# Order of the first levels' steps on ScalarE and VectorE during the dv products, in a transformer layer on one core

## Chip, cores and metric

The kernel runs on one core of one Trainium2 chip. The metric is the device time of one execution in microseconds; lower is better. The time before is the median of three runs.

## The reference, cut to what matters

The reference is two transformer blocks on 512 tokens of width 1024. The first has a projection `project(modulate(x, ...), w_in)` of the tokens and of 256 context tokens, cut into queries, keys and values of a gated linear attention (GLA, four heads) and of a differential attention (four heads; dq, dk, dv). The change lies in the GLA part, at the time that the kernel makes dv:

```python
def gla_chunk_scan(q, k, v, g, s0):
    ...
        qc, kc, vc, gc = inp
        cum = jnp.cumsum(gc, axis=2)
        o_inter = jnp.einsum('bhcd,bhde->bhce', qc * jnp.exp(cum), state)
        rel = cum[:, :, :, None, :] - cum[:, :, None, :, :]
        decay = jnp.exp(jnp.where(mask[:, :, None], rel, -jnp.inf))
        attn = jnp.einsum('bhid,bhjd,bhijd->bhij', qc, kc, decay)
        o = o_inter + jnp.einsum('bhij,bhje->bhie', attn, vc)
        last = cum[:, :, -1:, :]
        state = jnp.exp(last[:, :, 0, :, None]) * state + jnp.einsum('bhcd,bhce->bhde', kc * jnp.exp(last - cum), vc)
    ...
```

Both directions of the scan are computed. A score needs a decay that depends on the query and on the key. The kernel works in windows of 128 tokens and halves them in seven levels: at each level the decay from a key to a query in the other half goes through the border of the halves, and is a product of one factor for the key and one for the query, so that the scores of the level are an ordinary matrix product.

## The kernel before, in words

**Products.** TensorE (PE) runs nearly all the time on products of float32 values that are each split in a high and a low part (three matmuls for one). Weights come in units of up to 128x1024 values. SyncE's queue loads a unit into one of four buffers `raw` (line 537) once VectorE has done with the unit four before. ScalarE (ACT) makes the high part (`hi`, line 590), VectorE (DVE) the low part (`lo`, line 1350), two units ahead of PE. These calls stand between the other steps of each engine's program, whose order is written out by hand; each engine works strictly through its own list, and semaphores tie the lists together.

**The dv stage.** `tokens("dv", 2n, ...)` for n = 0 to 3 is one turn each: 36 matmuls of 128x512 (lines 2367 to 2369), two groups of 18. Between them PE has small work for the GLA part, and all of it goes through the PSUM banks 6 and 7, so that each small step waits until the one before has been read out of these two banks:

- after 12 matmuls of turns 1, 2 and 3: `item(j)`, the scores of a level. `item(0)` holds the undecayed scores of the window (line 2564) and the two lowest levels (line 2578); `item(1)` and `item(2)` (line 2564) are the next levels. An item waits for its level keys (semaphore `lmul`) and for banks 6 and 7.
- after 24 matmuls: `turn_keys(n)`, five transposes of decayed keys (line 2527). It waits for the readers of the item's scores.
- after 36 matmuls of turns 1 to 3: `state(n-1)`, twenty products of keys and values (line 2542). It waits for ACT's copies of the turned keys.

**What reads the banks.** The scores of `item(0)` are copied by ACT into the array `AT` (`first_scores`, line 744, two copies). Those of the later items are written over a part of `AT` by DVE under a mask (`item_scores`, line 1585, two predicated copies). The turned keys are copied by ACT (`turned_keys`, lines 737 and 738). The state is read by DVE (`state`, lines 1553 and 1559, five steps).

**What makes a level.** DVE takes four differences of running sums (`level_gaps`, lines 1509 to 1512, tile `Db`), ACT takes an exponential of them (`decays`, line 708), and DVE multiplies by queries and keys (`level_keys`, lines 1570 and 1573, tile `QKl`). Beside it, keys for the state are decayed (`key_decay` on ACT, line 702; `keys_decayed` on DVE, lines 1518 and 1519). `GAPS_AT[n]` is level n + 2, so the differences and the exponential of level n + 2 stand in turn n.

**The order before**, in turns 1 to 3:

- ACT, turn 1: `hi`, `decays(3)`, `first_scores(0)`, `turned_keys(1)`, `key_decay(3)`. Turns 2 and 3: `hi`, `decays(n + 2)`, `turned_keys(n)`.
- DVE, turn 1: `level_gaps(3)`, `lo`, `state(0)`, `keys_decayed(2)`, `level_keys(2)`. Turn 2: `level_gaps(4)`, `lo`, `level_keys(3)`, `item_scores(1)`, `state(1)`, `keys_decayed(3)`. Turn 3: `level_gaps(5)`, `lo`, `level_keys(4)`, `item_scores(2)`, `state(2)`.

After turn 3 ACT copies dv's six banks to `Vd` (line 762), and the dk products follow (lines 2333 to 2335).

Of the kernel before, what the change touches and what calls it, by code (L numbers as in the profile page):

```python
# [194 lines left out]
def build(nc, ap, out):  # L195
# [6 lines left out]
    with ctx:  # L202
# [55 lines left out]
        def bank(b, n=512, c=0):  # L258
            return pall[:, 512 * b + c:512 * b + c + n]
# [8 lines left out]
        def win(a):  # L268
            return a.rearrange("p (w t) -> p w t", t=128)
# [128 lines left out]
        for (_, _, _, cn, _, nk, _) in plan:  # L398
            offs.append(offs[-1] + 128 * cn * nk)
# [81 lines left out]
        ITEM_AT = {1: 0, 2: 1, 3: 2, 4: 3, 5: 4, 6: 5, 8: 6, 9: 7, 10: 8, 11: 9, 12: 10, 13: 11}  # L481
# [5 lines left out]
        def level_at(i):  # L487
            hp, lev = i // 7, i % 7 + 1
            return hp, lev, i % 2 if i < 6 else 2 + i % 2, NI * hp + max(lev - MG, 0)
# [85 lines left out]
        def _(e):  # L575
# [10 lines left out]
            def hi(upto):  # L586
                for j in range(made[0], min(upto + 1, NU)):
                    w.wait_ge(s_raw[j % 4], 16 * (j // 4 + 1))
                    w.wait_ge(s.used, j - 2)
                    e.activation(whi[j % 3][:, 0:cols(j)], raw[j % 4][:, 0:cols(j)], ACT.Copy).then_inc(s.hi, 1)  # L590
                    made[0] = j + 1
# [103 lines left out]
            def key_decay(i):  # L695
                z, hp = i // 2, i % 2
                if z == 0:
                    w.wait_ge(s.kds, hp + 1)
                    e.activation(ktd[:, hp, :], ktd[:, hp, :], ACT.Exp, scale=GN).then_inc(s.kde, 1)
                else:  # L700
                    w.wait_ge(s.kt, hp + 1)
                    e.activation(ktd[:, hp, :], Fc[:, 1, hp, :], ACT.Exp, scale=GN).then_inc(s.kde, 1)

            def decays(i):
                t = level_at(i)[2]
                w.wait_ge(s.lsub, i + 1)
                use_exp()
                e.activation(Db[t][:, :, :], Db[t][:, :, :], ACT.Exp, scale=GN).then_inc(s.lexp, 1)
# [25 lines left out]
            def turned_keys(i):  # L734
                z, hp = i // 2, i % 2
                w.wait_ge(s.kt, i + 1)
                e.activation(ktok[z][:, 0:4, hp, :], win(bank(6)), ACT.Copy).then_inc(s.ktk, 1)
                e.activation(ktok[z][:, 4, hp, :], bank(7, 128), ACT.Copy).then_inc(s.ktk, 1)

            def first_scores(hp):  # L740

                for sub in range(2):
                    w.wait_ge(s.lp, 2 * NI * hp + sub + 1)
                    e.activation(AT[hp][:, sub, :], bank(6 + sub), ACT.Copy, scale=2.0).then_inc(s.lat, 1)
# [3 lines left out]
            for n in range(4):  # L748
                hi(J[("dv", 2 * n)] + 2)
                if n == 0:  # L750
                    turned_keys(0)
                for i in GAPS_AT[n]:
                    decays(i)
                if n == 1:
                    first_scores(0)
                if n:
                    turned_keys(n)
                if n < 2:
                    key_decay(2 + n)
# [29 lines left out]
            for i in range(4):  # L789
                n = 4 + i  # L790
# [42 lines left out]
            for i in range(4):  # L833
                n = 8 + i
# [506 lines left out]
        def _(e):  # L1341
# [4 lines left out]
            def lo(upto):  # L1346
                for j in range(made[0], min(upto + 1, NU)):
                    w.wait_ge(s.hi, j + 1)
                    n = cols(j)
                    e.tensor_tensor(wlo[j % 3][:, 0:n], raw[j % 4][:, 0:n], f(whi[j % 3][:, 0:n]),  # L1350
                                    ALU.subtract).then_inc(s.lo_v, 1)
                    made[0] = j + 1
# [140 lines left out]
            def level_gaps(i):  # L1493
                hp, lev, t, _ = level_at(i)
                D_ = Db[t]
                b = 64 >> (lev - 1)

                def pr(x):
                    return x.rearrange("p (n t b) -> p n t b", t=2, b=b)

                F_, E_ = pr(Fc[:, 0, hp, 0:512]), pr(Fc[:, 1, hp, 0:512])
                rf = F_[:, :, 0, b - 1:b].to_broadcast([128, 256 // b, b])
                rb = E_[:, :, 1, 0:1].to_broadcast([128, 256 // b, b])
                Dq, Dk = pr(D_[:, 0, :]), pr(D_[:, 1, :])
                w.wait_ge(s.tot, 2 + 2 * hp)
                if i >= 6:
                    w.wait_ge(s.up, 4)
                w.wait_ge(s.lmul, i - 1)
                e.tensor_tensor(Dq[:, :, 1, :], F_[:, :, 1, :], rf, ALU.subtract)
                e.tensor_tensor(Dq[:, :, 0, :], rb, E_[:, :, 0, :], ALU.subtract)  # L1510
                e.tensor_tensor(Dk[:, :, 0, :], rf, F_[:, :, 0, :], ALU.subtract)
                e.tensor_tensor(Dk[:, :, 1, :], E_[:, :, 1, :], rb, ALU.subtract).then_inc(s.lsub, 1)

            def keys_decayed(i):
                hp = i % 2
                w.wait_ge(s.kde, i + 1)
                w.wait_ge(s.dn, 4)
                e.tensor_tensor(ktd[:, hp, 0:512], ktd[:, hp, 0:512], qk[:, hp, 1, :], ALU.mult)
                e.tensor_tensor(ktd[:, hp, 512:768], ktd[:, hp, 512:768], kc[:, hp, :], ALU.mult).then_inc(s.kdm, 1)
# [27 lines left out]
            def state(i):  # L1547
                z, hp = i // 2, i % 2
                order = windows[z]
                w.wait_ge(s.up, i + 1)  # L1550
                w.wait_ge(s.dec, 1)
                own = S_[:, z, hp, order[2], :]
                e.tensor_copy(own, bank(6, 128)).then_inc(s.stv, 1)
                for k in range(1, 5):
                    to = own if k == 1 else S_[:, z, hp, order[k + 1], :]
                    frm = own if k <= 2 else S_[:, z, hp, order[k], :]
                    add = bank(6, 128, 128 * k) if k < 4 else bank(7, 128)
                    w.wait_ge(s.stv, 5 * i + k)
                    e.scalar_tensor_tensor(to, frm, dect[:, z, hp, order[k]:order[k] + 1], add, ALU.mult,
                                           ALU.add).then_inc(s.stv, 1)  # L1560

            def level_keys(i):
                hp, lev, t, _ = level_at(i)
                w.wait_ge(s.lexp, i + 1)
                if i >= 2:
                    w.wait_ge(s.lp, 2 * level_at(i - 2)[3] + 2)
                w.wait_ge(s.gq, 2)
                if lev <= MG:

                    e.scalar_tensor_tensor(QKl[t][:, :, :], Db[t][:, :, :], math.sqrt(0.5), qk[:, hp, :, :], ALU.mult,  # L1570
                                           ALU.mult).then_inc(s.lmul, 1)
                else:
                    e.tensor_tensor(QKl[t][:, :, :], Db[t][:, :, :], qk[:, hp, :, :], ALU.mult).then_inc(s.lmul, 1)

            def item_scores(j):
                hp, k = j // NI, j % NI
                if k == 0:
                    return
                for sub in range(2):
                    src, dst = win(bank(6 + sub)), win(AT[hp][:, sub, :])  # L1580
                    w.wait_ge(s.lp, 2 * j + sub + 1)
                    w.wait_ge(s.g_const, 3)
                    w.wait_ge(s.lat, 2 * (j - 1) + sub + 1)
                    m = lmask[:, MG + k - 1, :].unsqueeze(1).to_broadcast([128, 4, 128])
                    e.copy_predicated(dst, m, src).then_inc(s.lat, 1)

            keys_decayed(1)
            for n in range(4):
                if n:
                    for i in GAPS_AT[n]:  # L1590
                        level_gaps(i)
                lo(J[("dv", 2 * n)] + 2)
                if n == 0:
                    level_keys(0)
                    level_keys(1)
                    level_gaps(2)
                if n >= 2:
                    level_keys(n + 1)
                    item_scores(ITEM_AT[n])
                if n:  # L1600
                    state(n - 1)
                if 1 <= n < 3:
                    keys_decayed(n + 1)
                if n == 1:
                    level_keys(2)


            def query_gap(hp):
# [23 lines left out]
            for i in range(4):  # L1632
                n = 4 + i
# [44 lines left out]
            for i in range(4):  # L1678
                n = 8 + i
# [24 lines left out]
            for i in range(4):  # L1704
                n = 12 + i
# [191 lines left out]
            for i in range(4):  # L1897
                lo(J[("zu", i, 0)] + 2)
                w.wait_ge(s.vf, 4 + i + 1)
                cur, n = u[:, i, :], 0  # L1900
# [8 lines left out]
                n = 2 << i  # L1909
# [1442 lines left out]
```

## Time and profile before

| what | us |
|---|---|
| median of three runs (1601.65 to 1602.03) | 1601.9 |
| the profiled execution | 1601.25 |
| span of the profiled execution | 1599.4 |
| PE busy in the span | 1548.7 |
| VectorE busy | 930.6 |
| ScalarE busy | 733.1 |
| GpSimd busy | 120.9 |

The span is the time between the first and the last instruction of the profiled execution; 1.85 us lie around it. The table shows which engine is nearly full. A busy time says nothing about one stage, though: what a step costs is seen in the timeline, where each row is one instruction or some equal ones in a row, and where brackets tell how long the engine stood idle ahead of it and what released it. The rows of the last section are of that kind. The dv stage with the change lies between 118 and 159 us.

### The profile page before, as it was taken

The page shows a single profiled execution, that of the slowest core. Times are in us where ns is not written, and L with a number is a line of the kernel's source. Part 1 is how long each engine was busy: PE and PEld are TensorE (multiplying, and loading weights), DVE is VectorE, ACT ScalarE, POOL GpSimd, SP SyncE. Part 2 cuts the span into 40 slices and gives each one's busy share as a digit, 9 for nine tenths or more (in the row PEclk, how much of TensorE's full clock was granted, in tenths as well). Part 3 has the DMA queues.
Part 4 walks back from the last instruction along what each step waited for, and adds up shares of the span by engine and source line. Part 5 has one row for each costly group of instructions (what it writes and reads, how often), then busy time and mean ns, then how long its engine had stood idle before and what let it go on. Part 6 is the DMA issues. An engine that isn't in the chain of part 4 may idle for free.

```text
span 1599.4 us, 19834 instructions
## 1 busy us (share of the span) xinstructions
PE 1548.7 (97%) x7939; PEld 1250.4 (78%) x7939; DVE 930.6 (58%) x1405; ACT 733.1 (46%) x1158; POOL 120.9 (8%) x89
## 2 busy tenths in 40 slices
PE   8998998989999999999999899999989999999998
PEld 5676876778788888888778677788779888888887
DVE  4765878876644433334646555365757785267745
ACT  5463546774432222323443667455556553244432
POOL 0000214630000000000100111130010000000000
PEclk9999999899999999999999999999999999999999
DMA  9721112105333232223232222143313232333221
GB/s 380 273 93 54 53 54 61 46 4 194 119 132 119 82 121 100 92 68 104 90 109 63 67 73 69 40 145 93 92 44 102 68 118 74 111 106 103 79 86 63
DMA packets 49840, 157.70 MB, mean 99 GB/s; under 512 B 5682, under 2 KB 12466, under 8 KB 49492
## 3 DMA queue, kind: packets, MB, share of 16 engines
q1 hardware_dynamic: 48352, 151.80, 28.9%
q10 hardware_dynamic: 1396, 4.63, 0.8%
q8 instruction: 63, 1.03, 0.3%
q14 instruction: 29, 0.24, 0.0%
HBM read 154.31 MB, written 2.10 MB: 98 GB/s over the span
## 4 chain that ended last, share of the span: by engine, by line
PE 78%; DVE 12%; ACT 8%; issue 2%; POOL 0%; DMA 0%; DVEq 0%; SPq 0%; ACTq 0%
PE pall L2333 18%; PE pall L2334 17%; PE pall L2335 17%; PE pall L2893 2%; PE pall L2894 2%; PE pall L2895 2%; PE pall L2367 1%; PE pall L2368 1%; PE pall L2369 1%; DVE wlo L1350 1%; ACT whi L590 1%; ACT e L908 1%; DVE R L1363 1%; DVE statd L1727 1%; DVE W L1361 1%
## 5 line engine op out<-in xcount | busy, mean ns | idle before, releaser
L1350 DVE TENSOR_TENSOR wlo<-raw,whi 128x1024 fp32r<-128x1024 f32 (+2 forms) x263 | 294.2, 1119 | 291.2 <-ACT whi L590 291.1
L590 ACT ACTIVATE whi<-raw 128x1024 fp32r<-128x1024 f32 (+2 forms) x263 | 247.0, 941 | 179.6 <-PE pall L2335 164.6
L2333 PE MATMUL pall<-h5h,whi 128*128 128x512 f32 x320 | 124.9, 390 | 1.0 <-DVE wlo L1350 1.0
L2335 PE MATMUL pall<-h5h,wlo 128*128 128x512 f32 x320 | 124.5, 389 | 0.0
L2334 PE MATMUL pall<-h5l,whi 128*128 128x512 f32 x320 | 124.5, 389 | 0.0
L2333 PE MATMUL pall<-h2h,whi 128*128 128x512 f32 x320 | 124.5, 389 | 0.0
L2334 PE MATMUL pall<-h2l,whi 128*128 128x512 f32 x320 | 124.5, 389 | 0.0
L2335 PE MATMUL pall<-h2h,wlo 128*128 128x512 f32 x320 | 124.5, 389 | 0.0
L2333 PEld LDWEIGHTS pall<-h5h,whi 128*128 128x128 f32 x320 | 60.1, 188 | 14.1 <-DVE wlo L1350 1.4
L2334 PEld LDWEIGHTS pall<-h2l,whi 128*128 128x128 f32 x320 | 60.1, 188 | 12.6
L2335 PEld LDWEIGHTS pall<-h5h,wlo 128*128 128x128 f32 x320 | 60.1, 188 | 12.5
L2333 PEld LDWEIGHTS pall<-h2h,whi 128*128 128x128 f32 x320 | 60.1, 188 | 12.5
L2335 PEld LDWEIGHTS pall<-h2h,wlo 128*128 128x128 f32 x320 | 60.1, 188 | 12.4
L2334 PEld LDWEIGHTS pall<-h5l,whi 128*128 128x128 f32 x320 | 60.1, 188 | 12.3
L2333 PE MATMUL pall<-fh,whi 128*128 128x512 f32 x176 | 68.5, 389 | 0.0
L2334 PE MATMUL pall<-fl,whi 128*128 128x512 f32 x176 | 68.5, 389 | 0.0
L2335 PE MATMUL pall<-fh,wlo 128*128 128x512 f32 x176 | 68.5, 389 | 0.0
L2333 PE MATMUL pall<-ch,whi 128*128 128x512 f32 x154 | 59.9, 389 | 0.0
L2334 PE MATMUL pall<-cl,whi 128*128 128x512 f32 x154 | 59.9, 389 | 0.0
L2335 PE MATMUL pall<-ch,wlo 128*128 128x512 f32 x154 | 59.9, 389 | 0.0
L996 ACT ACTIVATE fh<-tmp 128x512 fp32r<-128x512 f32 x22 | 13.9, 632 | 95.1 <-DVE tmp L1833 95.1
L2893 PE MATMUL pall<-h3h,whi 128*128 128x512 f32 x120 | 49.6, 414 | 0.3 <-ACT tmp L1071 0.3
(519 smaller groups left out, 3677.6 us busy)
## 6 DMA issues: line engine op xcount, KB each, us to landing
raw<-in_weights SPq DMA_DIRECT2D x204, 512.0 KB, 3.5
mraw<-in_wmod SPq DMA_DIRECT2D x32, 512.0 KB, 4.9
mod<-in_weights SPq DMA_DIRECT2D x16, 512.0 KB, 14.7
raw<-in_weights SPq DMA_DIRECT2D x25, 256.0 KB, 2.6
raw<-in_weights SPq DMA_DIRECT2D x32, 192.0 KB, 2.3
xT<-in_x SPq DMA_DIRECT2D x4, 512.0 KB, 5.4
xT<-in_x ACTq DMA_DIRECT2D x1, 2048.0 KB, 7.6
out_y<-xT SPq DMA_DIRECT2D x5, 256.0 KB, 2.2
```

What stands on the lines that cost most here:

```text
L590: e.activation(whi[j % 3][:, 0:cols(j)], raw[j % 4][:, 0:cols(j)], ACT.Copy).then_inc(s.hi, 1)
L908: e.activation(EB[n % 3][c][:, :], bank(b, 768), ACT.Exp, bias=sd[:, col + 1:col + 2], accum_out=sd[:, col + 2:col + 3]).then_inc(s.ex, 1)
L1350: e.tensor_tensor(wlo[j % 3][:, 0:n], raw[j % 4][:, 0:n], f(whi[j % 3][:, 0:n]), ALU.subtract).then_inc(s.lo_v, 1)
L1361: e.scalar_tensor_tensor(W[:, 0:n], m, EPS * dim, W[:, 0:n], ALU.add, ALU.mult).then_inc(s.rsum, 1)
L1363: e.scalar_tensor_tensor(r, W[:, 0:n], 1.5, r, ALU.subtract, ALU.mult, reverse0=True).then_inc(s.rstd, 1)
L1727: e.reduce_max(sd[:, col + 1:col + 2], bank(2 * dpair[c, n], 768), AX.X, negate=True).then_inc(s.mx, 1)
L2333: e.matmul(o_, a[:, kk, :], xh(k), start=(k == 0), stop=False)
L2334: e.matmul(o_, a[:, kk, :], xl(k), start=False, stop=False)
L2335: mm = e.matmul(o_, b[:, kk, :], xh(k), start=False, stop=(k == nk - 1))
L2893: e.matmul(bank(b), a[:, k, :], xh[:, k, :], start=(k == 0), stop=False)
L2894: e.matmul(bank(b), a[:, k, :], xl[:, k, :], start=False, stop=False)
L2895: mm = e.matmul(bank(b), c[:, k, :], xh[:, k, :], start=False, stop=(k == nk - 1))
```

## The change

It changes no instruction, only the order of some within ACT's and DVE's lists. On ACT, `first_scores(0)` goes ahead of `decays(3)` in turn 1. On DVE, `item_scores(n - 1)` of turns 2 and 3 goes from behind `level_keys` to the head of the turn, ahead of `level_gaps` and `lo`; and `level_keys(2)` of turn 1 goes ahead of `state(0)`. (`ITEM_AT` gives item 1 for turn 2 and item 2 for turn 3.)

```diff
@@ ScalarE
                 if n == 0:
                     turned_keys(0)
+                if n == 1:
+                    first_scores(0)
                 for i in GAPS_AT[n]:
                     decays(i)
-                if n == 1:
-                    first_scores(0)
                 if n:
                     turned_keys(n)
                 if n < 2:
@@ VectorE
             keys_decayed(1)
             for n in range(4):
+                if n >= 2:
+                    item_scores(ITEM_AT[n])
                 if n:
                     for i in GAPS_AT[n]:
                         level_gaps(i)
@@
                     level_keys(0)
                     level_keys(1)
                     level_gaps(2)
-                if n >= 2:
+                else:
                     level_keys(n + 1)
-                    item_scores(ITEM_AT[n])
-                if n:
                     state(n - 1)
                 if 1 <= n < 3:
                     keys_decayed(n + 1)
-                if n == 1:
-                    level_keys(2)
```

## Rows read from the trace of the kernel before

**Rows 1.** The page: PE's, VectorE's and ScalarE's busy time, instructions; weight loads to landing.

```profile
PE 1548.7 (97%) x7939; PEld 1250.4 (78%) x7939; DVE 930.6 (58%) x1405; ACT 733.1 (46%) x1158; POOL 120.9 (8%) x89
...
raw<-in_weights SPq DMA_DIRECT2D x204, 512.0 KB, 3.5
```

**Rows 2.** Stretches: busy us of PE, PEld, DVE, ACT, POOL; granted clock; DMA share, GB/s.

```profile
118.00:159.00 41.00, 36.51 (x330) 28.57 (x328) 23.94 (x45) 14.17 (x23) 0.00 (x0) 1.00 0.16 53
276.00:292.00 16.00, 13.95 (x50) 10.01 (x50) 13.44 (x18) 8.47 (x17) 9.08 (x7) 0.68 0.36 131
```

**Rows 3.** Timeline of PE, dv turns 0 and 1: start us, length, instruction, idle before.

```profile
114.78 0.39 PE L2369 MATMUL pall<-whi,hxl 128*128 128x512 f32 x1
115.01 0.71 PE L2527 MATMUL pall<-ident,ktd 128*128 128x128 f32 x5
115.47 0.47 PE L2367 MATMUL pall<-whi,hxh 128*128 128x512 f32 x1
...
126.16 0.39 PE L2369 MATMUL pall<-whi,hxl 128*128 128x512 f32 x1
128.28 0.74 PE L2527 MATMUL pall<-ident,ktd 128*128 128x128 f32 x5 [1.74 <-ACT AT L744]
128.78 0.48 PE L2367 MATMUL pall<-whi,hxh 128*128 128x512 f32 x1
```

**Rows 4.** Timeline of PE, dv turn 2.

```profile
135.55 0.39 PE L2369 MATMUL pall<-whi,hxl 128*128 128x512 f32 x1
137.09 1.16 PE L2564 MATMUL pall<-QKl 64*128 64x128 f32 x16 [1.15 <-DVE QKl L1573]
...
140.81 0.39 PE L2369 MATMUL pall<-whi,hxl 128*128 128x512 f32 x1
142.02 0.74 PE L2527 MATMUL pall<-ident,ktd 128*128 128x128 f32 x5 [0.83 <-DVE AT L1585]
142.52 0.48 PE L2367 MATMUL pall<-whi,hxh 128*128 128x512 f32 x1
...
145.43 1.31 PE L2542 MATMUL pall<-Vg,ktok 128*64 128x128 f32 x20
```

**Rows 5.** Timeline of PE, dv turn 3.

```profile
149.29 0.39 PE L2369 MATMUL pall<-whi,hxl 128*128 128x512 f32 x1
149.61 1.16 PE L2564 MATMUL pall<-QKl 64*128 64x128 f32 x16
...
153.33 0.39 PE L2369 MATMUL pall<-whi,hxl 128*128 128x512 f32 x1
154.51 0.73 PE L2527 MATMUL pall<-ident,ktd 128*128 128x128 f32 x5 [0.79 <-DVE AT L1585]
155.00 0.47 PE L2367 MATMUL pall<-whi,hxh 128*128 128x512 f32 x1
```

**Rows 6.** Timeline of ScalarE, dv turn 1.

```profile
126.18 1.04 ACT L708 ACTIVATE Db<-Db 128x1024 f32<-128x1024 f32 x1
127.12 1.06 ACT L744 ACTIVATE AT<-pall 128x512 f32<-128x512 f32 x2
129.06 0.60 ACT L737 ACTIVATE ktok<-pall 128x512 f32<-128x512 f32 x1 [0.88 <-PE pall L2527]
```

**Rows 7.** Timeline of VectorE, end of dv turn 1 and turn 2.

```profile
133.05 0.29 DVE L1553 COPY S_<-pall 128x128 f32<-128x128 f32 x1 [5.51 <-PE pall L2542]
133.37 1.50 DVE L1559 SCALAR_TENSOR_TENSOR S_<-S_,tots,pall 128x128 f32<-128x128 f32 x4
...
135.72 1.22 DVE L1573 TENSOR_TENSOR QKl<-Db,qk 128x1024 f32<-128x1024 f32 x1
136.98 0.42 DVE L1509 TENSOR_TENSOR Db<-Fc 128x256 f32<-128x256 f32 x1
...
138.32 1.22 DVE L1350 TENSOR_TENSOR wlo<-raw,whi 128x1024 fp32r<-128x1024 f32 x1
...
140.59 1.33 DVE L1585 COPY_PREDICATED AT<-lmask,pall 128x512 f32<-128x512 uint8 x2
```

## The prediction

> **What bounds the kernel.** I read the page first: PE is busy 97% of the span, the next engine 58% [rows 1]. So a change that touches only ScalarE's and VectorE's order can pay only where PE stands still for them. The second view is the busy time by stretch: in the dv stage, 118 to 159 us, PE works 36.5 of 41 us, at the full granted clock, with DMA 16% busy [rows 2]. Some 4.5 us of standing still are there to be had. The third view is PE's timeline of that stage. It shows four waits of size, at three kinds of work that all go through the banks 6 and 7 [rows 3 to 5]. The fourth and fifth are the timelines of ScalarE and VectorE at the same moments, which show what each releaser was doing before it released [rows 6, 7].
>
> **What a wait costs.** Without a wait the transposes start 0.23 us behind the last matmul, and the next matmul starts 0.46 us behind them (114.78, 115.01, 115.47) [rows 3]. An item starts 0.32 us behind its matmul (149.29, 149.61) [rows 5]. Against this:
>
> - transposes, turn 1: the next matmul at 128.78, and 126.16 + 0.23 + 0.46 = 126.85 without a wait: 1.93 us [rows 3];
> - item 1, turn 2: 137.09 against 135.55 + 0.32 = 135.87: 1.22 us [rows 4];
> - transposes, turn 2: 142.52 against 140.81 + 0.69 = 141.50: 1.02 us [rows 4];
> - transposes, turn 3: 155.00 against 153.33 + 0.69 = 154.02: 0.98 us [rows 5].
>
> In all 5.15 us; the change aims at each of the four.
>
> **Part 1, the first copies ahead of the exponential (ScalarE).** Before, ScalarE starts the exponential of level 3 at 126.18 and the two copies at 127.12. They end at 128.18, and PE's transposes start 0.10 later [rows 3, 6]. The scores are ready long before: the item ran ahead of the 12 matmuls that end the group at 126.16. With the copies first they take the slot from 126.18, end at 127.24, and the transposes start at 127.34 in place of 128.28. Gain 0.94 us; 0.99 of the wait stays, because ScalarE is not free before 126.18. The exponential now ends at about 128.2. Behind it are the copies of the turned keys, which wait for the transposes anyway (127.34 + 0.74 = 128.08), so they start at about 128.15 against 129.06 [rows 3, 6] and keep the gain. Cost on the path: nothing, covered by the transposes; were they done sooner, it would be the exponential's 1.04 at most. The moved exponential feeds level 3's keys, which are wanted ten microseconds later.
>
> **Part 2, level 2's keys ahead of the state (VectorE).** VectorE stands idle 5.51 us ahead of the state at 133.05 [rows 7]. The keys need 1.22 us, and their exponential stands in turn 0, so they fit into the idle time whole and cost nothing. Item 1 on PE, which waited for these keys (they end at 136.94), is then held only by the state's steps, which read the banks: they end at 133.37 + 1.50 = 134.87 before [rows 7], 133.93 after part 1. Item 1 comes at 135.87 - 0.94 = 134.93, 1.0 us behind that, so its whole wait of 1.22 goes. Shift so far 2.16 us.
>
> **Part 3, the masked selections at the head (VectorE).** In turn 2 the selection of item 1 stood behind level 3's differences, the low part of a weight unit and the level's keys, and ended at 140.59 + 1.33 = 141.92, 0.1 ahead of the transposes [rows 4, 7]. Now it waits at the head for item 1: 134.93 + 1.16 = 136.09, plus 0.06 for the signal, and ends at about 137.5. The 12 matmuls end their group so that the transposes can start at 140.81 - 2.16 + 0.23 = 138.88: no wait, with 1.4 us to spare. Gain 1.02, shift 3.18. In turn 3 the same: item 2 at 149.61 - 3.18 = 146.43, selection over by 149.0, transposes at 150.38. Gain 0.98, shift 4.16 us.
>
> **What queues behind the new wait.** The selection is now a wait at the head of the list, and the differences of level 4, a weight unit's low part, and level 3's keys stand behind it. They start at 137.4 instead of 136.98 [rows 7]. The four differences end at 137.4 + 1.43 = 138.8, the exponential (1.06) at 139.9, and ScalarE's copies of the turned keys (0.85, start of the first to end of the second, the second not shown: bounds 0.60 and 1.20, for one or two copies of the length shown [rows 6]) at 140.5 to 141.1. PE wants them for the state at 145.43 - 3.18 = 142.25 [rows 4]. At least 1.1 us remain. Level 3's keys end at about 141.1 and are wanted at 146.4. The low part ends near 140 in place of 139.54, for the first dk unit. PE wanted that at about 159.2 (155.00, plus the 2.91 from transposes to state in turn 2, plus the state's 1.31 [rows 4, 5]), and will at about 155. SyncE's next load waits for that low part and starts 0.4 us later; a load lands 3.5 us after its issue [rows 1], four units ahead of PE. No moved step issues a DMA, and GpSimd has no work in the stage [rows 2].
>
> **Sum.** 0.94 + 1.22 + 1.02 + 0.98 = 4.16 us off the profiled execution's 1601.25, which gives 1597.1. The median of the runs stands 0.65 higher, and I take the gain from it: 1601.9 - 4.2 = 1597.7. At the end of the stage every engine has moved by the same 4.2 us: ScalarE's copies to `Vd`, the last state and the dk products all wait for PE's last dv matmul. So the later stages should keep the shift.
>
> **A clock that could take it or double it.** Between 276 and 292 us the granted clock averages 0.68 [rows 2]. Between the levels 1.0 and 0.5 that is 16 x 0.32 / 0.5 = 10.2 us at the lower one, 1.2 GHz, and PE had stood still several times just before. PE-bound work there loses up to half of it, 5.1 us. The Trainium skill ("TensorE: Matmul & The Clock Gate", "What's actually happening") says that the gate judges PE's activity by its own running time and does not restart with the kernel. By that rule a stage reached 4.2 us sooner could meet the gate otherwise, and the sum could be anything from -9.3 to +0.9. Against a large effect stands that the three runs agree within 0.38 us, so the stretch seems to cost the same each time; I leave the sum at -4.2.
>
> **Rivals.**
>
> 1. *The new head of the turn makes the exponential and the state late.* For it: three steps now hang on PE's item. Against it: 1.1 us of room even at the slow bound. If that room is overrun in both turns so that the 2.0 us of part 3 are given back, 2.16 remain: 1599.7. Chance 0.09.
> 2. *The change does not do what it says, or the gain is absorbed.* A wait put down to the selection could have had a second cause as late, or a later stage with a fixed date could wait longer. The only thing with dates of its own is DMA, at 16% here [rows 2]. Time 1601.9. Chance 0.05.
> 3. *The clock, on the other side.* The stretch at the lower level, now met 4.2 us sooner, grows, or another of PE's waiting stages falls into one. One more stretch of 10.2 us costs 5.1: 1601.9 - 4.2 + 5.1 = 1602.8, slower than before. It decides from 8.3 us more at the lower level on. Two such stretches would give 1607.9. Chance 0.03 for one, 0.02 for two.
> 4. *The clock, in favour.* The stretch does not occur: 1597.7 - 5.1 = 1592.6. Chance 0.03.
>
> **How the numbers follow.** The forecast has 0.78; its own range is 1596.7 (all 5.15 us gone) to 1598.7 (a quarter of the gain lost in signals and pitches). About 0.2%, or 3.2 us, is what a measurement of this kernel can tell from no change. Faster by more than that: forecast and rival 4, 0.81. Within: rivals 1, 2 and the single stretch of 3, 0.17. Slower: 0.02. The range reaches down from 1596.7 by a quarter of the clock's 5.1, to 1595.4, and up to rival 1 with 0.4 for the spread of runs, 1600.1; outside are rivals 2 to 4, some 0.13.
>
> **What would show it.** In the changed profile: transposes of turn 1 still wait, for about 0.8 us, for the copies (line 744), now ahead of the exponential (line 708). Item 1 and the transposes of turns 2 and 3 show no wait. VectorE stands idle at the head of turns 2 and 3, released by line 2564, some 1.2 us. The first dk matmul comes at about 155.1 in place of 159.2. The granted clock between 272 and 288 looks as before between 276 and 292. The prediction is wrong if PE waits ahead of the states (line 2542), if the first dk matmul comes later than 156, or if it comes at 155 and the end does not follow.

## The result, and the profile after

The changed kernel takes 1597.32 us in the median of 8 runs (1595.63 to 1597.57); the kernel before, run beside it, 1601.96 (8 runs, 1601.65 to 1602.74). The ratio is 0.9969, with a 95% interval of 0.9960 to 0.9977: faster by about 0.3%, or 4.6 us, and beyond the 0.2% that the prediction named as the limit. In microseconds the interval reaches from 3.7 to 6.4. The profiled execution took 1597.36 us, with a span of 1595.5 against 1599.4.

The page of the changed kernel, the line that answers to the first of [rows 1]:

```profile
PE 1549.6 (97%) x7939; PEld 1251.3 (78%) x7939; DVE 930.7 (58%) x1405; ACT 732.9 (46%) x1158; POOL 120.5 (8%) x89
```

Its busy time by stretch, the line that answers to the first of [rows 2] (busy us of PE, PEld, DVE, ACT, POOL, then granted clock, DMA share, GB/s):

```profile
118.00:159.00 41.00, 40.21 (x363) 32.09 (x363) 26.37 (x51) 17.42 (x28) 0.00 (x0) 1.00 0.17 53
```

No engine does more or less work over the span, and the granted clock of the stage is 1.00 in both kernels, so the gain there is not one of the clock. In the same 41 us PE is now busy for 40.21 us with 363 matmuls, where it was busy for 36.51 with 330. (The dv products end sooner now, so some of the 363 are dk products.) What is left of its standing still is one wait. PE's timeline, against [rows 3 to 5]:

```profile
115.68 0.71 PE L2525 MATMUL pall<-ident,ktd 128*128 128x128 f32 x5
...
126.83 0.39 PE L2367 MATMUL pall<-whi,hxl 128*128 128x512 f32 x1
128.01 0.74 PE L2525 MATMUL pall<-ident,ktd 128*128 128x128 f32 x5 [0.79 <-ACT AT L744]
...
135.28 0.39 PE L2367 MATMUL pall<-whi,hxl 128*128 128x512 f32 x1
135.59 1.16 PE L2562 MATMUL pall<-QKl 64*128 64x128 f32 x16
...
139.32 0.39 PE L2367 MATMUL pall<-whi,hxl 128*128 128x512 f32 x1
139.55 0.71 PE L2525 MATMUL pall<-ident,ktd 128*128 128x128 f32 x5
...
142.94 1.31 PE L2540 MATMUL pall<-Vg,ktok 128*64 128x128 f32 x20
...
150.86 0.39 PE L2367 MATMUL pall<-whi,hxl 128*128 128x512 f32 x1
151.09 0.71 PE L2525 MATMUL pall<-ident,ktd 128*128 128x128 f32 x5
...
155.78 0.47 PE L2331 MATMUL pall<-hxh,whi 128*128 128x512 f32 x1
```

and the first dk matmul of the kernel before:

```profile
159.21 0.47 PE L2333 MATMUL pall<-hxh,whi 128*128 128x512 f32 x1
```

PE's lines have moved up by two (2527 is now 2525). This execution comes to the stage 0.67 us later than the one of before (115.68 against 115.01), so times are to be compared from there. Item 1 stands 0.31 behind its matmul, the transposes of turns 2 and 3 0.23 behind theirs: no waits. Only the transposes of turn 1 still wait for `first_scores`. From turn 0's transposes to the first dk matmul it was 159.21 - 115.01 = 44.20 us before and is 155.78 - 115.68 = 40.10 now: 4.10 us, where the prediction had 4.16. I call this length the **stage** in what follows; it is how the experiments are compared, since what lies outside it varies by more: over the ten profiles of this document, PE comes to the stage after 114.4 to 116.0 us, and what follows the stage takes between 1439.4 and 1445.6 us. For this pair the span's 3.9 us are 4.10 less in the stage, 0.67 more ahead of it and about 0.5 less behind it.

ScalarE's timeline of the changed kernel, turn 1 and turn 2, against [rows 6]:

```profile
126.85 1.06 ACT L744 ACTIVATE AT<-pall 128x512 f32<-128x512 f32 x2
127.80 1.06 ACT L708 ACTIVATE Db<-Db 128x1024 f32<-128x1024 f32 x1
128.78 0.60 ACT L737 ACTIVATE ktok<-pall 128x512 f32<-128x512 f32 x1
...
139.48 1.06 ACT L708 ACTIVATE Db<-Db 128x1024 f32<-128x1024 f32 x1 [6.85 <-DVE Db L1512]
140.45 0.58 ACT L737 ACTIVATE ktok<-pall 128x512 f32<-128x512 f32 x1
140.93 0.27 ACT L738 ACTIVATE ktok<-pall 128x128 f32<-128x128 f32 x1
```

VectorE's, end of turn 1 and turn 2, against [rows 7]:

```profile
128.12 1.22 DVE L1573 TENSOR_TENSOR QKl<-Db,qk 128x1024 f32<-128x1024 f32 x1
132.77 0.29 DVE L1553 COPY S_<-pall 128x128 f32<-128x128 f32 x1 [3.43 <-PE pall L2540]
...
136.79 1.36 DVE L1585 COPY_PREDICATED AT<-lmask,pall 128x512 f32<-128x512 uint8 x2 [1.26 <-PE pall L2562]
138.03 0.41 DVE L1509 TENSOR_TENSOR Db<-Fc 128x256 f32<-128x256 f32 x1
```

Level 2's keys now sit in VectorE's idle time ahead of the state, and VectorE now stands idle for 1.26 us at the head of the turn, released by PE's item, which costs nothing. ScalarE's copies of the turned keys are over at 141.20, and PE's state begins at 142.94: 1.7 us of room for the chain behind the new wait.

### The profile page after: what moved, and what is told of

It is laid out like the page before. It is cut to its first block, busy times and chain, and to the rows that moved or that the text cites. A ratio compares the mean times of both kernels' runs of the same rounds, so it can differ in the third digit from the quotient of the medians.

```text
span 1595.5 us, 19834 instructions
## 1 busy us (share of the span) xinstructions
PE 1549.6 (97%) x7939; PEld 1251.3 (78%) x7939; DVE 930.7 (58%) x1405; ACT 732.9 (46%) x1158; POOL 120.5 (8%) x89
## 4 chain that ended last, share of the span: by engine, by line
PE 78%; DVE 11%; ACT 8%; issue 2%; POOL 0%; DMA 0%; DVEq 0%; SPq 0%; ACTq 0%
PE pall L2331 18%; PE pall L2333 18%; PE pall L2332 18%; PE pall L2891 2%; PE pall L2365 2%; PE pall L2367 2%; PE pall L2366 2%; PE pall L2893 2%; PE pall L2892 2%; DVE wlo L1350 1%; ACT whi L590 1%; ACT e L908 1%; DVE statd L1725 1%; DVE W L1361 1%; DVE R L1363 1%
```

## The experiments

Eight kernels, the first four on one chip, the other four together on one chip again. On the first chip the runs scattered more (the kernel before: 1600.71 to 1604.26 in 35 runs) than single parts of 1 to 2 us are worth, so the verdict on a part is read from its profile, and the runs stand beside it.

**Part 1 alone.**

```diff
 # the kernel before, ScalarE, turn 1
                 if n == 0:
                     turned_keys(0)
+                if n == 1:
+                    first_scores(0)
                 for i in GAPS_AT[n]:
                     decays(i)
-                if n == 1:
-                    first_scores(0)
```

> Only part 1: the two first copies ahead of the exponential on ScalarE, VectorE's order as before. My account: the transposes of turn 1 come 0.94 us sooner and every later wait stays as it was (1.22 at item 1, 1.02 and 0.98 at the transposes of turns 2 and 3), so PE's first dk matmul comes 0.94 sooner: -0.9 us in the trace and in the runs. Rival (the waits hand over to each other): item 1 still waits for level 2's keys, whose date hangs on something that did not move, and the shift at the dk products is 0.

PE's waits in the stage, 118 to 160 us (who waited, for whom, us in total, how often, the longest):

```profile
PE pall L2527 <- DVE AT L1585: 1.6, 2, 0.8
PE pall L2564 <- DVE QKl L1573: 1.1, 1, 1.1
PE pall L2527 <- ACT AT L744: 0.8, 1, 0.8
```

One wait has shrunk from 1.74 to 0.8, the three others stand as they were. The stage takes 159.26 - 115.99 = 43.27 us: 0.93 off, as expected, and nothing is handed on. The runs (1600.29 against 1601.54, ratio 0.9996, 0.9986 to 1.0005) cannot tell this from no change. The profiled execution itself took 1606.73 us, and what it lost, it lost behind the stage; see the last section.

**Part 2 alone.**

```diff
 # the kernel before, VectorE, turns 1 to 3
+                if n == 1:
+                    level_keys(2)
                 if n:
                     state(n - 1)
                 if 1 <= n < 3:
                     keys_decayed(n + 1)
-                if n == 1:
-                    level_keys(2)
```

> Only part 2: level 2's keys ahead of the state, selection behind level_keys as before, ScalarE as before. My account: item 1 loses its wait of 1.22 us, the transposes of turns 2 and 3 keep theirs (about 1.0 each): -1.2 us. Rival (hand over): the transposes of turn 2 wait 1.2 us longer, since the selection is held by work of VectorE with a fixed date: 0.

The same view:

```profile
PE pall L2527 <- ACT AT L744: 1.7, 1, 1.7
PE pall L2527 <- DVE AT L1585: 1.6, 2, 0.8
```

Item 1's wait is gone, the others are untouched. Stage 157.97 - 115.00 = 42.97: 1.23 off. Runs 1599.85 against 1601.54, ratio 0.9993 (0.9984 to 1.0001): in line with 1.2 us, but not shown by them.

**Part 3 alone.**

```diff
 # the kernel before, VectorE
             for n in range(4):
+                if n >= 2:
+                    item_scores(ITEM_AT[n])
                 if n:
                     for i in GAPS_AT[n]:
                         level_gaps(i)
...
                 if n >= 2:
                     level_keys(n + 1)
-                    item_scores(ITEM_AT[n])
```

> Only part 3: the selections at the head of turns 2 and 3, ScalarE and level 2's keys as before. My account: item 1 waits 1.2 us as before, the transposes of turns 2 and 3 no longer wait: -2.0 us. Rival (the new head of the turn makes the exponential late): PE waits ahead of the states (line 2542) of turns 2 and 3 and the gain is under 1 us, or a loss.

The same view (this file has one line more, so PE's lines are one further down):

```profile
PE pall L2528 <- ACT AT L744: 1.7, 1, 1.7
PE pall L2565 <- DVE QKl L1573: 1.1, 1, 1.1
```

The two waits for the selection are gone, and PE does not wait ahead of a state. Stage 157.24 - 114.94 = 42.30: 1.90 off, 0.1 less than expected. The tenth is spread over both turns (0.96 and 0.94 for 1.02 and 0.98). Runs 1599.65 against 1601.54, ratio 0.9991 (0.9982 to 1.0001).

**Parts 1 and 2.** The edits of the first two experiments together.

> Parts 1 and 2 without the selections at the head. My account: the parts add, 0.94 + 1.22 = 2.16 us off, with waits of about 1.0 us left at the transposes of turns 2 and 3. Rival: they overlap, and one of the two is worth less than 0.5 beside the other.

The same view:

```profile
PE pall L2527 <- DVE AT L1585: 1.6, 2, 0.8
PE pall L2527 <- ACT AT L744: 0.8, 1, 0.8
```

Stage 157.31 - 115.29 = 42.02: 2.18 off. The parts add: 0.93 + 1.23 = 2.16, and with part 3's 1.90 they give 4.06, against 4.10 for all together. The runs (1600.98, ratio 0.9995, 0.9986 to 1.0003) lie higher than the stage says. They reach from 1598.31 to 1603.95 and don't decide anything; that the clock, below, is behind this is not shown.

**The room behind the new wait, two doses.** Products that nobody reads lengthen the chain behind the selection in turns 2 and 3.

```diff
 # the changed kernel, level_gaps (VectorE); the smaller dose has tmp[2:]
                 w.wait_ge(s.lmul, i - 1)
+                for t_ in (tmp[0:] if i in (4, 5) else ()):
+                    e.tensor_tensor(t_[:, :], qk[:, 0, 0, :], qk[:, 0, 1, :], ALU.mult)
                 e.tensor_tensor(Dq[:, :, 1, :], F_[:, :, 1, :], rf, ALU.subtract)
```

> The changed kernel with two more VectorE products of 128x512 (into tmp[2] and tmp[3], which nothing reads) behind the selection and ahead of the differences of levels 4 and 5: the chain selection, differences, exponential, copies of the turned keys is made 1.2 us longer in each of turns 2 and 3. In the changed kernel the copies ended at 141.20 and PE's state began at 142.94, so about 1.6 us of room. My account: hidden, the first dk matmul at the same place as with the change (4.1 us ahead of before, counted from turn 0), no wait ahead of line 2540's counterpart. Rival (the wait at the head of the turn has used the room up): PE waits ahead of the states, 1.2 us per turn, 2.4 in all.

> As before, but four such products per turn, 2.4 us. My account: the room of 1.6 is overrun by 0.8 us in each of the two turns, PE waits ahead of the states of turns 2 and 3 for ScalarE's copies, and the gain of 4.1 at the dk products falls to about 2.5. Rival (the chain is not what ends the state's wait; something else holds it or nothing does): the gain stays 4.1.

PE's waits with the smaller dose:

```profile
PE pall L2527 <- ACT AT L744: 0.8, 1, 0.8
```

and with the larger:

```profile
PE pall L2542 <- ACT ktok L738: 1.5, 2, 0.7
PE pall L2527 <- ACT AT L744: 0.8, 1, 0.8
```

In the profile the two added products take 1.2 us of VectorE's time and the four 2.4. The smaller dose is hidden whole: stage 154.79 - 114.69 = 40.10, the changed kernel's to the hundredth. With the larger, a new wait stands ahead of each of the two states, for ScalarE's copies of the turned keys, as rival 1 described it. The stage is 156.13 - 114.42 = 41.71, so 1.61 of the gain is lost, 0.8 per turn; the gain is 2.49, expected about 2.5. Rival 1 is thus a real mechanism: by these figures it bites once the chain grows by more than some 1.6 us (2.4 less the 0.8 lost), and the change leaves that room. Each dose was run once, with 1597.01 us for the smaller and 1600.37 for the larger: 3.4 us apart where the stages differ by 1.6, so a single run does not measure the dose.

**The copies moved further up.**

```diff
 # the changed kernel, ScalarE
             for n in range(4):
+                if n == 1:
+                    first_scores(0)
                 hi(J[("dv", 2 * n)] + 2)
                 if n == 0:
                     turned_keys(0)
-                if n == 1:
-                    first_scores(0)
```

> The changed kernel with the first copies moved further up, ahead of the high part of a weight unit too, to the head of turn 1. My account: the wait of 0.98 us that was left at turn 1's transposes goes, since ScalarE is free 0.95 earlier; the high part, the low part and level 2's keys come 1.0 later and stay inside VectorE's idle time ahead of the state (3.43 us in the changed kernel). The first dk matmul comes 5.1 us ahead of before, 1.0 ahead of the changed kernel: about 1596.3. Rival (the wait is handed on): item 1 or the state of turn 1 now waits, and the shift at the dk products stays 4.1.

PE's timeline:

```profile
115.95 0.71 PE L2525 MATMUL pall<-ident,ktd 128*128 128x128 f32 x5
...
127.10 0.39 PE L2367 MATMUL pall<-whi,hxl 128*128 128x512 f32 x1
127.33 0.74 PE L2525 MATMUL pall<-ident,ktd 128*128 128x128 f32 x5
...
155.10 0.47 PE L2331 MATMUL pall<-hxh,whi 128*128 128x512 f32 x1
```

and ScalarE's:

```profile
126.16 1.07 ACT L744 ACTIVATE AT<-pall 128x512 f32<-128x512 f32 x2
127.11 1.06 ACT L590 ACTIVATE whi<-raw 128x1024 fp32r<-128x1024 f32 x1
128.06 1.06 ACT L708 ACTIVATE Db<-Db 128x1024 f32<-128x1024 f32 x1
```

The last wait is gone too, and VectorE's idle time ahead of the state falls from 3.43 to 1.52 us, the cover that pays for it. Stage 155.10 - 115.95 = 39.15: 5.05 off the kernel before, 0.95 off the changed one. The runs show the gain over the kernel before: 1596.28 us (5 runs, 1595.07 to 1597.06), ratio to the kernel before 0.9959 (0.9945 to 0.9972). The changed kernel on the same chip took 1597.37, which is 1.1 us more; its runs (1596.84 to 1597.59) overlap with these, and the lead over it rests on the stage's 0.95 us. By the stage this version beats both.

**The changed kernel again.** No edit.

> The changed kernel once more, on the same chip as the three others. My account: the first dk matmul 4.1 us ahead of before, counted from turn 0, as in its first profile, since this part holds no chance. What comes behind it moves by the length of time at the lower clock, which differs from run to run: the time lies 4.1 below the kernel before, give or take the clock's 3 us in a single run, and in the median of the rounds within 1 us of that. Rival (the stage's gain depends on the run): the shift at the dk products differs by more than 0.5 us from 4.1.

Stage 154.65 - 114.55 = 40.10, the same to the hundredth. Runs 1597.37 us (5 runs, 1596.84 to 1597.59) against 1601.84 (9 runs): ratio 0.9967 (0.9954 to 0.9979).

## Why the prediction was right

- **Bound and waits.** PE's standing still in the stage was the place, and each of the four waits went as its row said. The three single-part kernels give 0.93, 1.23 and 1.90 us where the text had 0.94, 1.22 and 2.00. Part 3's tenth is the only difference in a gain that can be seen; what takes it was not tested.
- **The wait that stays.** Forecast about 0.8 us by the view's count; the changed kernel shows 0.79. The cause named, ScalarE not free before 126.18, is right: it makes a unit's high part until then, as is shown by the version that moves the copies ahead of that too and loses the wait.
- **The work queued behind the new wait.** Forecast: hidden, with 1.1 to 1.7 us of room; the profile has 1.7. (The two copies take 0.75 us, 140.45 to 141.20, where the sum had 0.85 with bounds of 0.60 and 1.20.) The doses of 1.2 and 2.4 us bracket it: the first costs nothing, the second 0.8 per turn.
- **The stage's sum.** 4.10 against 4.16.
- **The whole.** The median fell by 4.6 us, 0.5 more than the stage. The interval of 3.7 to 6.4 us holds the stage's 4.1, so the runs do not show that there is anything more to explain. What lies outside the stage varies by more than half a microsecond from profile to profile.
- **What the text had wrong.** The step on the clock said that the slow stretch near 280 us "seems to cost the same each time", because three runs agreed within 0.38 us, and that it would look as before. It does not: the stretch of 272 to 288 us of the changed kernel, which answers to the second of [rows 2], reads

```profile
272.00:288.00 16.00, 14.81 (x43) 10.90 (x44) 12.99 (x18) 7.81 (x15) 9.46 (x7) 0.57 0.36 131
```

  a granted clock of 0.57 in place of 0.68; the kernel's second profile has 0.79 there. The sum was not hurt, since other stretches went the other way, as the rows of the last section show. That they balanced in the profiled execution is luck: the step left the clock out of the sum for a reason that did not hold.
- **The rivals.** Rival 2 (nothing) is out by the interval. Rival 1 needs some 1.6 us more work per turn to bite at all. Rivals 3 and 4 described something real: the time at the lower clock does change. But it changes between executions of one kernel too, and in the 13 runs of the changed kernel on record the time stays between 1595.63 and 1597.59 us. The largest effect seen, 5.5 us, was in the kernel with part 1 alone.

## What to carry to other kernels

When one engine is nearly full and its waits are for a bank to be read out, look at what the reading engine does just before the read: an instruction there that nobody needs soon can change places with the read, and the gain is the length of that instruction, up to the wait. Moving a waiting instruction to the head of a list is free as long as the chain that it now holds up ends ahead of its own reader; work out that room from the timeline, and test it with a dose of idle work. Where parts are worth a microsecond in 1600, compare the length of one stage in the profiles, not the time of the runs.

## What the runs showed of the hardware that was not expected

The granted clock falls to its lower level (0.5, 1.2 GHz) in some stages, but not in the same ones each time, though the program is the same. In the changed kernel's first profile, for one, PE was busy for 4.97 of the 7.5 us from 267.5 to 275 us, the clock fell at the end of that, and then it read

```profile
277.50:280.00 2.50, 2.50 (x8) 1.55 (x9) 2.21 (x4) 1.29 (x3) 1.27 (x1) 0.50 1.01 433
```

Standing still alone does not tell where it falls: in the dv stage of the kernel before PE stood still for 4.5 of 41 us, and the clock stayed at 1.00 [rows 2]; between 1200 and 1230 us PE is busy for 29.3 to 29.5 of 30 us in all three profiles below, and the clock fell in two of them. The kernel before, four stretches (columns as in the stretches above):

```profile
265.00:300.00 35.00, 30.19 (x147) 21.67 (x144) 30.73 (x43) 23.84 (x43) 19.55 (x13) 0.85 0.25 87
325.00:350.00 25.00, 22.37 (x156) 18.81 (x155) 21.61 (x34) 16.43 (x31) 9.40 (x6) 1.00 0.00 1
885.00:910.00 25.00, 21.49 (x98) 15.51 (x100) 12.87 (x28) 14.77 (x29) 1.83 (x2) 0.93 0.19 58
1200.00:1230.00 30.00, 29.47 (x191) 26.75 (x190) 22.81 (x48) 20.90 (x47) 0.00 (x0) 0.94 0.30 97
```

The changed kernel in its first profile:

```profile
265.00:300.00 35.00, 31.49 (x130) 22.41 (x128) 29.57 (x43) 25.59 (x47) 20.23 (x15) 0.80 0.21 75
325.00:350.00 25.00, 22.35 (x143) 18.75 (x142) 19.30 (x31) 16.98 (x32) 8.83 (x5) 0.93 0.01 2
885.00:910.00 25.00, 21.61 (x111) 15.65 (x110) 14.23 (x31) 16.37 (x30) 1.83 (x2) 1.00 0.20 64
1200.00:1230.00 30.00, 29.32 (x207) 26.61 (x206) 23.78 (x50) 19.73 (x45) 0.00 (x0) 1.00 0.25 76
```

The very same kernel in its second:

```profile
265.00:300.00 35.00, 29.16 (x140) 21.25 (x140) 30.12 (x44) 25.50 (x47) 20.59 (x14) 0.90 0.21 75
325.00:350.00 25.00, 22.88 (x163) 19.50 (x162) 20.93 (x34) 17.58 (x35) 9.31 (x6) 1.00 0.01 2
885.00:910.00 25.00, 22.27 (x116) 16.59 (x118) 13.21 (x27) 14.76 (x27) 1.83 (x2) 0.93 0.20 64
1200.00:1230.00 30.00, 29.47 (x197) 27.03 (x196) 24.41 (x52) 19.71 (x47) 0.00 (x0) 0.94 0.26 79
```

In the first profile the clock fell between 325 and 350 us and stayed full in the two later stretches; in the second it is the other way round. The time at the lower level in the first stretch is 35 x 0.20 / 0.5 = 14 us in the one and 7 us in the other. This agrees with what the Trainium skill says ("TensorE: Matmul & The Clock Gate", "What's actually happening"), that the gate's timing does not restart with the kernel and so differs from run to run. The two executions also came to the dv stage 1.1 us apart (115.68 and 114.55); no run here shows that the gate's timing alone makes the difference.

How much it can be worth is seen in the kernel with part 1 alone:

```profile
265.00:300.00 35.00, 31.69 (x133) 22.45 (x129) 29.68 (x42) 21.89 (x39) 18.63 (x12) 0.76 0.24 87
325.00:350.00 25.00, 22.25 (x129) 18.16 (x129) 17.93 (x28) 16.15 (x31) 7.83 (x5) 0.86 0.00 1
```

Its span was 1604.9 us, 5.5 above the kernel before, although it had come to the end of the stage level with it (159.26 against 159.21). It came to the stage 0.98 us later and gained 0.93 in it, so all but 0.1 of the 5.5 was lost behind the stage. Against the kernel before, the two stretches hold (0.09 x 35 + 0.14 x 25) / 0.5 = 13.3 us more at the lower level; at half speed that is an estimate of up to 6.6 us lost, and 5.5 were. Such an execution hides a gain of 4 us completely. Whether the order of the steps has a part in this is open: 11 of the 52 runs of the kernel before took 1603.5 us or more, two of the 12 with part 1 alone over 1606.7, and none of the 13 of the changed kernel over 1597.6.
